# Expert tokens by one gather of whole rows, results stored densely and gathered by token, routing weights in the closing sums

## What is computed

```python
def hier_moe(h, w_rg, w_re, w_gate, w_up, w_down):
    ...
    weights = pg_top * top_p                 # (tokens, 2)
    expert = grp * EXP_PER_GROUP + top_i     # 32 experts, two per token
    ...
    def run_block(args):
        tok, e = args
        xb = x_pad[tok]
        hb = jax.nn.silu(xb @ w_gate[e]) * (xb @ w_up[e])
        return hb @ w_down[e]
    ...
    y = jax.ops.segment_sum(yb * slot_w[:, None].astype(yb.dtype), slot_tok, num_segments=t + 1)[:t]
```

## Time and profile before

| | us |
|---|---|
| median of 3 runs | 1517.57 (1515.67 to 1518.67) |
| span of the profiled execution | 1574.3 |
| mixer stage with start (in that execution) | 0 to about 885 |
| routing, up to the first gate-up product | about 885 to 916.7 |
| expert stage | 916.7 to 1525.5 |
| closing sums, norm, stores | 1525.5 to 1574.3 |

### The profile page before, as it was taken

One profiled execution on the slowest core, in us unless ns is written; L12 is line 12 of the kernel. 1 busy time (PEld: TensorE's weight loads), 2 busy tenths in 40 slices (PEclk: granted clock), 3 DMA queues, 4 the chain that ended last, 5 costly groups with the idle time before them and its releaser, 6 DMA issues.

```text
span 1574.3 us, 37571 instructions
## 1 busy us (share of the span) xinstructions
PE 1458.9 (93%) x15114; PEld 912.2 (58%) x15114; DVE 692.5 (44%) x1951; ACT 464.2 (29%) x1315; POOL 246.9 (16%) x319
## 2 busy tenths in 40 slices
PE   7989999999999999999987489999999999999994
PEld 4555665656656656566555256666666666666651
DVE  1664773846737648477386731111111111111116
ACT  2831924527428245173271000001000000000002
POOL 0000001001000010010000032333333333333320
PEclk9999999999999999999986689999999999999997
DMA  9945655556456465574540549999999999999857
GB/s 374 393 149 178 232 167 202 168 180 223 165 187 210 155 211 166 173 254 140 194 175 1 200 167 391 368 360 353 357 357 356 357 372 356 357 357 357 341 205 309
DMA packets 57390, 402.20 MB, mean 255 GB/s; under 512 B 10376, under 2 KB 10568, under 8 KB 35440
## 3 DMA queue, kind: packets, MB, share of 16 engines
q1 hardware_dynamic: 42224, 363.72, 62.4%
q0 software_dynamic: 15104, 37.80, 6.4%
HBM read 380.87 MB, written 29.36 MB: 261 GB/s over the span
## 4 chain that ended last, share of the span: by engine, by line
PE 80%; DVE 11%; issue 4%; ACT 3%; DMA 2%; POOL 0%; DVEq 0%; SPq 0%; POOLq 0%; ACTq 0%
PE ps L778 24%; PE ps L550 23%; PE ps L796 11%; DVE big L1107 5%; PE duo L705 3%; PE ps L705 3%; PE ps L486 2%; PE ps L662 1%; PE duo L766 1%; DMA big<-in_w_in 1%; PE duo L512 1%; PE duo L504 1%; ACT xin L920 1%; PE ps L728 1%; PE duo L786 1%
## 5 line engine op out<-in xcount | busy, mean ns | idle before, releaser
L778 PE MATMUL ps<-big 128*32 128x256 f32 x6144 | 381.8, 382 | 8.3 <-DVE big L1107 2.1
L778 PEld LDWEIGHTS ps<-big 128*32 128x32 f32 x6144 | 254.4, 110 | 125.9 <-issue 61.2
L550 PE MATMUL ps<-big,xin 128*128 128x386 f32 (+1 forms) x672 | 272.7, 543 | 0.4 <-DMA big<-in_w_in 0.4
L550 PE MATMUL ps<-big 128*128 128x512 f32 (+2 forms) x608 | 210.6, 498 | 11.0 <-DMA big<-in_w_in 11.0
L796 PE MATMUL ps<-big 128*32 128x256 f32 x3072 | 182.4, 380 | 1.9 <-ACT big L1063 0.9
L1107 DVE TENSOR_TENSOR big<-big 128x256 f32<-128x256 f32 (+5 forms) x294 | 158.1, 561 | 57.6 <-ACT big L886 35.0
L1541 DVE SCALAR_TENSOR_TENSOR big<-big,ps 128x128 f32<-128x128 f32 x96 | 27.6, 288 | 343.8 <-ACT big L1059 340.6
L550 PEld LDWEIGHTS ps<-big,xin 128*128 128x128 f32 x672 | 122.7, 194 | 90.1 <-issue 48.9
L550 PEld LDWEIGHTS ps<-big 128*128 128x128 f32 x608 | 113.2, 192 | 88.4 <-issue 70.5
L796 PEld LDWEIGHTS ps<-big 128*32 128x32 f32 x3072 | 100.9, 110 | 73.3 <-issue 17.0
L1059 ACT ACTIVATE big<-ps 128x128 f32<-128x128 f32 x96 | 26.6, 277 | 380.4 <-remote 198.6
(11 more groups left out here) (255 smaller groups left out, 1537.6 us busy)
## 6 DMA issues: line engine op xcount, KB each, us to landing
big<-in_w_in SPq DMA_DIRECT2D x64, 1024.0 KB, 4.8
big<-in_w_gate SPq DMA_DIRECT2D x32, 2048.0 KB, 7.7
big<-in_w_up SPq DMA_DIRECT2D x32, 2048.0 KB, 12.7
big<-in_w_down SPq DMA_DIRECT2D x32, 2048.0 KB, 7.9
big<-in_w_in SPq DMA_DIRECT2D x64, 772.0 KB, 4.6
big<-in_w_in SPq DMA_DIRECT2D x32, 512.0 KB, 4.4
hn_rows<-big POOLq DMA_DIRECT2D x8, 1024.0 KB, 6.9
big<-y_rows SPq DMA_DIRECT2D x8, 1024.0 KB, 11.9
```

The lines of the kernel that those rows point to most:

```text
L550: last = t_.matmul(ps[6 + n % 2][:, 0:w], x_src[:, k, :], wv[:, k % KH, :], start=k == 0, stop=k == KD - 1)
L778: last = t_.matmul(ps[GU[t]][TG * j:TG * (j + 1), 0:2 * HC], xT[:, k, TG * t:TG * (t + 1)], wgu[par][:, :, k, HC * j:HC * (j + 1)], start= ...
```

## The change

- `hn_rows` holds each token once. The slot numbers are found with 96-wide place rows (`in_pos`) and 55-wide block rows (`in_blk`), in one sum on 96 partitions; no quarters, no `rep`. Empty slots get a number beyond the bound and are skipped.
- A block's tokens come by one indirect DMA of 96 rows of 4 KB; the first two read their numbers straight from `slots`. `x_block` transposes eight pieces of 96x128, `x_gain2` has two steps of 384 columns.
- No weights in the slots: the second round of one-hots is gone, and `w12` (halved, for the tanh form of silu) is multiplied in at the end, by DVE in `summed`, by TensorE with `wdiag`, the identity times a weight column. `w12` is computed after `slots`.
- ScalarE stores `yo` densely to `y_rows` by block and slot, four DMAs a block (`y_store`), behind `h_copy`. `rows_stored` on GpSimd waits for both stores at the end of the loop body.
- At the end GpSimd gathers for each tile and each choice 128 rows of 4 KB from `y_rows` by `dsti`: sixteen indirect DMAs. As rows of blocks not run could be addressed, 22 spare blocks are filled with constants by SP during tile 1's loads (`fill_spare`).
- TensorE and ScalarE load the loop bound after block 0's first steps. Some semaphores share a name.

```diff
-        hn_v = hn_d.rearrange("(t p k) d -> t p k d", p=P, k=2)
+        hn_v = hn_d.rearrange("(t p) d -> t p d", p=P)
...
+        y_v = y_d.rearrange("(b t r) (j c) -> j r b t c", t=NG_B, r=TG, j=CT)
...
+            def fill_spare(b):
+                sp.dma_start(y_spare[:, b:b + 2, :], heads(cst[0:BLK, EARLY:EARLY + DM], 2)).then_inc(sem("y_filled"), 16)
...
             for n in range(NG):
                 load_w(1, n)
+                fill_spare(NE + 2 * n)
...
-            for n, rows in enumerate((in_grp, in_wgt)):
-                for r in range(4):
-                    pe.wait_ge(sem("dst_ready"), 4 * n + r + 1)
...
+            for r in range(CT):
+                pe.wait_ge(sem("dst_ready"), r + 1)
+                for k in range(CT * r, CT * r + CT):
+                    last = t_.matmul(ps[6][0:BLK, 0:N_BL], in_pos[:, k, :], in_blk[:, k, :], start=k == 0,
+                                     stop=k == 2 * NT - 1)
...
-                for k in range(2 * NG_B):
-                    last = t_.transpose(ps[k // 4][:, (k % 4) * P:(k % 4 + 1) * P], xg[par][:, k * P:(k + 1) * P],
-                                        ident)
+                for k in range(KD):
+                    last = t_.transpose(ps[k // 4][:, (k % 4) * BLK:(k % 4 + 1) * BLK],
+                                        xg[par][0:BLK, k * P:(k + 1) * P], ident[0:BLK, 0:BLK])
...
+            def y_store(b, par):
+
+                act.wait_ge(sem("y0_ready"), b + 2)
+                act.wait_ge(sem("y1_ready"), b + 2)
+                for j in range(CT):
+                    act.dma_start(y_v[j][:, bass.ds(b, 1), :, :].rearrange("r o t c -> r (o t) c"),
+                                  three(yo[par][TG * j:TG * (j + 1), :], NG_B, YC)).then_inc(sem(f"y_sent{par}"), 16)
...
-                    v.scalar_tensor_tensor(hact[:, t, :], eg[:, t, :], wslot[:, bass.ds(b * NG_B + t, 1)],
-                                           bank[:, HC:2 * HC], ALU.mult, ALU.mult) \
-                        .then_inc(sem("hact_ready"), 1)
+                    tt(hact[:, t, :], eg[:, t, :], bank[:, HC:2 * HC], ALU.mult).then_inc(sem("hact_ready"), 1)
...
-                cseq(tt(hrow, hrow, cm_y[t][:, 0:DM], ALU.add))
-                tt(hrow, hrow, cm_y[t][:, DM:2 * DM], ALU.add).then_inc(sem("c_sum"), 1)
+                seq(v.scalar_tensor_tensor(hrow, cm_y[t][:, 0:DM], w12[:, 0, t:t + 1], hrow, ALU.mult, ALU.add))
+                v.scalar_tensor_tensor(hrow, cm_y[t][:, DM:2 * DM], w12[:, 1, t:t + 1], hrow, ALU.mult, ALU.add) \
+                    .then_inc(sem("c_sum"), 1)
...
+            def rows_of(b, par, index):
+                g.indirect_dma_start(xg[par][0:BLK, :], None, hn_d, bass.IndirectOffsetOnAxis(ap=index, axis=0),
+                                     bounds_check=SEQ - 1, oob_is_err=False).then_inc(sem(f"tok_loaded{par}"), 16)
...
             with pool.Fori(1, pairs) as q:
-                gather(2 * q + 1, 1, False)
-                add_rows(2 * q - 2, q - 1, 0)
-                gather(2 * q + 2, 0, False)
-                rows_added(q - 1, 0)
-                add_rows(2 * q - 1, q - 1, 1)
-                rows_added(q - 1, 1)
...
+                gather(2 * q + 1, 1)
+                gather(2 * q + 2, 0)
+                rows_stored(q - 1, 0)
+                rows_stored(q - 1, 1)
...
+            for t in range(NT):
+                for k in range(2):
+                    g.indirect_dma_start(cm_y[t][:, DM * k:DM * (k + 1)], None, y_d,
+                                         bass.IndirectOffsetOnAxis(ap=dsti[:, k, t:t + 1], axis=0),
+                                         bounds_check=Y_ROWS - 1, oob_is_err=False).then_inc(sem(f"y_loaded{t}"), 16)
```

More of the change, by code:

```diff
@@ L45 @@
 NB_MIN = NE
-N_GR = (NB_MAX + 1) * NG_B
+N_BL = NB_MAX + 1
+Y_ROWS = NB_MAX * BLK
 GU = (2, 3, 7)
 N_CAP = 10
+NO_TOKEN = 4 * SEQ
 N_OVER = NB_MAX - NE
@@ L1528, in x_gain2 @@
                 dve.wait_ge(sem("xt_done"), b + 1)
[L1529 to L1533 removed]
+                for half in range(2):
+                    ks = slice(KH * half, KH * half + KH)
+                    last = tt(xT[:, ks, :], three(ps[half][:, 0:KH * BLK], KH, BLK), bc(g2c[:, ks], BLK), ALU.mult)
                 last.then_inc(sem("xT_ready"), 1)
@@ L1691, in rows_added, with rows_stored @@
+            def rows_stored(q, par):
+                pool.wait_ge(sem(f"y_sent{par}"), q * 16 * CT + 16 * CT)
                 pool.sem_inc(sem(f"y_free{par}"), 1)
-            gather(0, 0, True)
-            gather(1, 1, True)
+            pool.sem_inc(sem("gates"), 1)
+            for b in range(2):
+                rows_of(b, b, slots[0:BLK, b:b + 1])
             pool.wait_ge(sem("blk_ready"), 1)
```

244 lines of the change are left out of this document (95 added, 149 removed).

## The result

The change made the kernel slower: median 1558.2 us of four runs (1557.0 to 1562.4) against 1517.2 us, ratio 1.0279, 95% interval 1.0264 to 1.0294. The forecast was 1515.9 us, the range ended at 1524.

What follows compares the result with a forecast made beforehand. TensorE was taken to bound the expert stage, narrowly, at 17.2 us a block. Routing -7.4, transposes +7.0, transfers and mixer 0, end -1.3 summed to -1.7: 1515.9 us, range 1484 to 1524.

Steps and rivals of the forecast that it cites:

- What bounds the kernel: Expert stage: TensorE ends last, narrowly, at 17.2 us a block against 16.2 to 17.0 us of transfers.
- the stalls of the triplets: Expert stage: TensorE held by indirect-DMA triplets, about 58 us, mostly from recording; rival (real) 1470 us, chance 0.28.
- Routing, -7.4: From ranking products to first gate-up: shorter slot search and one direct gather start gate-up at 909.3, 7.4 us sooner.
- Transposes, +7.0: Each block on TensorE: eight transposes for six, weight load setting the distance, +0.22 us x 32; lower end 0.
- It now waits for y_sent of both blocks at the loop's end: GpSimd's loop: the gather behind this wait is due over 20 us later; no cost was counted.
- Transfers, 0: Expert stage: dense stores add 4.2 MB, 0.31 to 0.33 us a block, hidden while TensorE is last.
- transfers end last: Rival, expert stage: queues sustain less than 398 GB/s, so added bytes cost +11.8 us; 1520.7 us, chance 0.14.
- The limit of 358 GB/s: Expert stage: HBM to SBUF transfers held near 358 GB/s per core; by it the change comes out near 1521 us.
- ScalarE's stores, mixer stage, 0: ScalarE's four issues a block (1.3 to 2.2 us) find room; eleven mixer-stage fills cost 0, bound +2.
- End, -1.3: After the last down product: stores, then sixteen gathers, complete tile 1 at 1538.3, 1.3 us sooner; ends -4.5, +4.
- the signs that the prediction named for being wrong: Timed runs fall with the profiled span, gate-up waits for DMA, or the last sixteen gathers exceed 1.4 us each.

Runs made afterwards that it cites:

- b0: The kernel before, unchanged, timed and profiled once more: one timed run of 1516.0 us, profiled span 1514.4 us.
- a1: The changed kernel, but GpSimd waits for no store in the loop; ScalarE and VectorE wait for the landing themselves: 1521.4 us, ratio 1.0031.
- s4: The changed kernel, GpSimd's waits kept, with the gathers, transposes and gains of the kernel before: 1546.8 us, ratio 1.0217.
- a2: The changed kernel with the four dense stores issued by GpSimd in place of ScalarE, GpSimd's waits kept: 1535.3 us, ratio 1.0131.
- a3: The changed kernel with each partition's 3 KB of results stored to consecutive addresses: 1529.3 us, ratio 1.0091.
- a6: The changed kernel with ScalarE and VectorE waiting for the stores instead of GpSimd, and 3 KB per partition stored contiguously: 1529.7 us, ratio 1.0095.
- s3: The changed kernel with ScalarE and VectorE waiting for the stores instead of GpSimd, and the quarter-row gathers, transposes and gains of before: 1513.9 us, ratio 0.9982.
- h1: The changed kernel with scatters of 1 KB rows as before in place of dense stores; whole-row gathers stay: 1526.9 us, ratio 1.0058.
- h2: h1 with the gathers, transposes and gains of the kernel before (three indirect DMAs of 128 rows of 1 KB a block): 1512.2 us, ratio 0.9973.
- h4: h1 with each gather cut by columns into four of 96 rows of 1 KB: 1529.4 us, ratio 1.0074.
- s1: a1 with the tokens of a block spread over its 96 places: 1525.6 us, ratio 1.0063.
- h3: h1 with the tokens of a block spread over its 96 places: 1527.5 us, ratio 1.0069.
- h5: h1 with four copies on GpSimd, of about 1 us each, ahead of each whole-row gather: 1528.4 us, ratio 1.0087.
- h6: h1 with the gather cut into four of 96 rows of 1 KB and the tokens spread over the 96 places: 1522.5 us, ratio 1.0037.

## Why the prediction was wrong

**What bounds the kernel: right.** TensorE ends last at 17.2 us a block (550.1 / 32 = 17.2), and the stalls of the triplets are absent from an execution that took a timed run's time (b0). (The stage's mean rate, which the prediction gives as 357 GB/s, is 348 in the earlier trace rows; 357 is what most slices have. Nothing changes by it.) The judgement was better than its reason: it took them for a thing of every recording; they are a thing of one.

**Routing, -7.4: measured -5.6.** From the ranking products to the slots it came as summed (16.2 us against 16.3). The first gather, after GpSimd's long pause, took 1.65 us to issue, and its data landed 4.5 us after it began, not 2.9:

```profile
902.96 0.19 DVE L1484 CAST big<-big 96x55 int32<-96x55 f32 x1
...
904.58 1.65 POOL L1641 DMA_INDIRECT big<-hn_rows,big  x1 [22.54 <-issue]
...
909.11 0.90 PE L750 MATMUL duo<-cst,big 96*128 96x96 f32 x4 [6.43 <-DMA big<-hn_rows,big]
```

**Transposes, +7.0: measured 0.** Eight of 96 columns take 0.81 us from first start to the down product (1085.54 to 1086.35), six of 128 also 0.81 (940.38 to 941.19, above). Over the stage the transposes take 32.3 us in a1 and 32.2 in b0. The lower bound named was the right one: 8 x 96 = 6 x 128 moving columns. The starts lie 0.109 us apart with 128 moving columns and 0.083 with 96, in proportion to them. The mistake was to conclude from L728's 0.11 with 36 columns, a product that is no transpose, that the weight load sets the distance.

**"It now waits for y_sent of both blocks at the loop's end; behind it stands gather(2q+3), due over 20 us later": this is the step that failed.** The slack was right, even more: from the end of the down product of block 2q-1 to x_block(2q+3) 28 us pass (0.5 + 10.5 + 0.8 + 5.3 + 0.5 + 10.5). What has to fit in was never summed: copies and issue 0.8, landing of the store 19.7 from its first issue (1075.5 to 1095.2), row numbers and issue 1.6, landing of the gather 11.5, together 33.6, 5.5 too much. I priced a store's landing only for the idle end (2.8 us) and let the loop's stand at nothing, though 2 MB of weights on the same engines took 7.7 to 12.7 before (medians). a1 shows the price, 36.8 us, and s4 much the same with other gathers (33); a2, and a3 beside a6, show that it is a matter of a few us over the slack.

**Transfers, 0: the form of the gather was not seen.** The bytes were right: the dense stores' 4.2 MB more are hidden with quarter rows (s3, 397 GB/s and no wait for weights). That 96 whole rows are dearer than 3 x 128 quarter rows of the same bytes was in no term; it costs 7.5 us with dense stores (a1 to s3) and 14.7 with scatters (h1 to h2; 13 by the ratios, since their lots differ). The rival "transfers end last" named 1520.7 and a1 measured 1521.4, but not by its mechanism, a rate below 398 GB/s for whatever moves. The limit of 358 GB/s that the prediction weighed (the Trainium skill, "DMA: Bandwidth & Descriptors", section "Where 436 GB/s comes from") does not hold here, where one core runs: 392 in h2 and 397 in s3 over 540 us.

**ScalarE's stores, mixer stage, 0: right as far as they can be seen.** Four issues take 1.8 us, and the tanh behind them still waits 3.1 us for TensorE (1078.77). Of the fills, nothing shows above the scatter of the ranking products' start.

**End, -1.3: measured +0.2.** The first y gather starts 5.0 us after the last down product, sooner than the 5.9 predicted, but the gathers land 5.8 us (median) after issue where I took 3.0.

Put together, the small terms came to -5.4 us where -1.7 was forecast (-5.6, 0, +0.2 against -7.4, +7.0, -1.3); that they end so close is partly luck, since the 7.0 was wrong whole. The error of 42 us is two things in the loop that stood at nothing, 36.8 and 7.5. Of the signs that the prediction named for being wrong none looked at them: gate-up waited 1.3 us for DMA, and the sixteen last gathers came 1.3 us apart. The wait for tokens in x_block was on no list.

**Left open.** Why whole rows on 96 partitions slow the transfers beside them. The gather's form is shown to be the cause (h1 to h2, a1 to s3), the reason is not. It is neither the length of the rows alone (h4), nor their spread alone (s1, h3), nor the moment (h5); length and spread together may be a part (h6). A gather of whole rows on 128 partitions was not tried. The Trainium skill, "SBUF — State Buffer", section "Door 1: The DMA port swizzle", says that partitions 0 to 63 reach only eight of sixteen DMA ports, and "DMA: Bandwidth & Descriptors", section "The descriptor swizzle", that in a transfer to 128 partitions each engine writes one port of its own. By these rules 96 partitions would make engines cross at the ports, and about 64 rows in the first places fill half of them. That is an inference from the pages. No run here tests the crossing; the nine rows at once of after's first gather fit the second half, but with up to 15 at once (s1) the time did not fall.

## What to carry to other kernels

A wait moved to an engine with nothing to do is paid by what stands behind it: sum the whole loop from the wait's release to the use of what is queued behind (store landing, issue, gather landing) and compare with the slack, and take landings from the loaded stretch, never from the idle end. Let the one who overwrites a buffer wait for it. For small-packet stores beside large-packet loads, take (packets per engine) x (the large packet's time) as a first estimate of the landing: it gave 15.8 us where the packets passed in 16.0, though with a third of the packets the landing only fell from 11.9 to 9.1. And when a gather's form changes, compare the GB/s of the few us in which it moves, not only its bytes and instructions.

## What was not expected of the hardware

- One profiled execution of the same kernel spanned 1574.3 us, another 1514.4, with timed runs at 1516 to 1518. The longer had half-microsecond gaps beside each triplet of indirect DMAs, the other none.
- 96 rows of 4 KB gathered while weights stream: 279 GB/s in total in one window of 4 us; 384 rows of 1 KB, the same amount of data: 438 in another kernel's. (In both only the real slots move, about 64 of 96.)
- Transposes of 96 and of 128 columns cost by their moving columns, although a piece of 96 loads 128 columns as weights too: 0.81 us for eight and for six, starts 0.083 and 0.109 us apart.
